# Layer 0 of a two-block transformer kernel: the v blocks first, q and k by pairs of heads, the attention steps woven between their half blocks, and the head's first weights in column parts

## What is computed

```
cond = silu(c)                                    # c: (1, 1024)
mod = cond @ ada_w[0] + ada_b[0]                  # ada_w[0]: (1024, 6144)
sh1, sc1, g1, sh2, sc2, g2 = split(mod, 6)
h = rms_norm(x, norm1_g[0]) * (1 + sc1) + sh1
q, k, v = split(h @ diff_w_in, 3)                 # diff_w_in: (1024, 3072); 8 heads
s = q_m . k_m / 8   for the two maps m of a head  # 64 features each; ALiBi, chunk-causal mask
a = softmax(s_0) - lam * softmax(s_1)             # lam from four vectors of 64
o = rms_norm(a @ v, subln_g) * 0.2
x = x + g1 * (o @ diff_w_out)
h = rms_norm(x, norm2_g[0]) * (1 + sc2) + sh2
x = x + g2 * moe(h)                               # 32 experts, top 2, 6 MB of weights each
```

## Time and profile before

| what | value |
|---|---|
| median of 3 runs | 1855.09 us (1849.57 to 1863.38) |
| profiled execution | 1853.06 us |
| its span, first to last instruction | 1851.3 us |
| mean granted TensorE clock | 0.971 of full speed |
| busy PE / DVE / ACT / POOL | 91% / 26% / 24% / 9% of the span |
| DMA, whole span | 585 MB, mean 316 GB/s |

### The profile page before, as it was taken

One profiled execution on the slowest core, in us unless ns is written; L12 is line 12 of the kernel. 1 busy time (PEld: TensorE's weight loads), 2 busy tenths in 40 slices (PEclk: granted clock), 3 DMA queues, 4 the chain that ended last, 5 costly groups with the idle time before them and its releaser, 6 DMA issues.

```text
span 1851.3 us, 18408 instructions
## 1 busy us (share of the span) xinstructions
PE 1687.5 (91%) x7485; PEld 858.7 (46%) x7485; DVE 489.6 (26%) x931; ACT 444.1 (24%) x939; POOL 158.1 (9%) x235
## 2 busy tenths in 40 slices
PE   5997999889888878989999999999998899989988
PEld 2843543333333334835464444444443356565564
DVE  1357220000000103244241002221120123553362
ACT  2015221111111102015231112334331034343351
POOL 2012010000000010113000010000000000100000
PEclk9998999999989999999989999999998999999999
DMA  9999779999999999987369989999999962413310
GB/s 348 360 350 401 277 278 419 421 421 420 421 421 419 420 413 397 338 349 239 109 259 389 369 298 404 393 414 420 420 420 409 377 230 100 148 53 117 137 46 24
DMA packets 119488, 585.12 MB, mean 316 GB/s; under 512 B 11744, under 2 KB 16680, under 8 KB 94720
## 3 DMA queue, kind: packets, MB, share of 16 engines
q1 hardware_dynamic: 97776, 489.59, 66.0%
q0 software_dynamic: 21504, 88.72, 13.1%
q10 hardware_dynamic: 112, 5.51, 0.8%
HBM read 578.87 MB, written 21.32 MB: 324 GB/s over the span
## 4 chain that ended last, share of the span: by engine, by line
PE 58%; DMA 29%; DVE 6%; ACT 3%; issue 3%; SPq 1%; ACTq 0%; DVEq 0%
PE psum L2179 55%; DMA ring<-in_expert_w_up 20%; DMA work<-in_ada_w 4%; DMA ring<-in_diff_w_in 2%; DVE work L1859 1%; PE psum L697 1%; DMA ring<-in_expert_w_gate 1%; DMA work<-in_ctx 1%; DMA work<-in_w_mod 1%; DVE small L1055 1%; PE psum L2418 1%; PE psum L1196 1%; DMA ring<-in_w_out 0%; DVE work L2147 0%; DVE work L2074 0%
## 5 line engine op out<-in xcount | busy, mean ns | idle before, releaser
L2179 PE MATMUL psum<-ring,work 128*64 128x512 f32 (+5 forms) x4272 | 1092.6, 574 | 69.6 <-DMA ring<-in_expert_w_up 56.3
L2179 PEld LDWEIGHTS psum<-ring,work 128*64 128x64 f32 (+2 forms) x4272 | 422.7, 152 | 666.1 <-issue 638.0
L2179 PE MATMUL psum<-work 128*128 128x192 f32 (+9 forms) x1048 | 220.4, 375 | 8.5 <-DVE work L2007 3.0
L2179 PEld LDWEIGHTS psum<-work 128*128 128x128 f32 (+3 forms) x1048 | 146.5, 191 | 108.0 <-issue 86.9
L2074 DVE TENSOR_TENSOR work<-work,psum 128x256 f32<-128x256 f32 x64 | 26.9, 421 | 593.2 <-ACT work L1779 593.2
L1779 ACT ACTIVATE work<-psum 128x256 f32<-128x256 f32 x64 | 24.5, 383 | 607.4 <-PE psum L2179 607.4
L2179 PE MATMUL psum<-work,ring 128*128 128x256 f32 x704 | 156.1, 381 | 3.5 <-DMA ring<-in_diff_w_in 2.0
L2179 PEld LDWEIGHTS psum<-work,ring 128*128 128x128 f32 x704 | 132.0, 190 | 27.8 <-issue 7.0
L1646 ACT ACTIVATE work<-psum 128x256 f32<-128x256 f32 (+5 forms) x184 | 79.7, 443 | 225.0 <-PE psum L2418 76.0
L1545 POOL DMA_INDIRECT expert_rows<-work,targets x56 | 55.1, 984 | 807.1 <-DVE work L2100 807.1
L2100 DVE TENSOR_TENSOR work<-psum,rows 128x512 f32<-128x512 f32 x64 | 44.3, 692 | 255.8 <-PE psum L2179 255.7
(11 more groups left out here) (293 smaller groups left out, 956.3 us busy)
## 6 DMA issues: line engine op xcount, KB each, us to landing
ring<-in_expert_w_gate SPq DMA_DIRECT2D x60, 2048.0 KB, 16.5
ring<-in_expert_w_up SPq DMA_DIRECT2D x60, 2048.0 KB, 17.2
ring<-in_expert_w_down SPq DMA_DIRECT2D x57, 2048.0 KB, 13.5
work<-in_ada_w POOLq DMA_DIRECT2D x40, 1024.0 KB, 8.0
ring<-in_w_in SPq DMA_DIRECT2D x12, 2048.0 KB, 8.8
work<-in_w_mod POOLq DMA_DIRECT2D x16, 1024.0 KB, 7.9
ring<-in_diff_w_in SPq DMA_DIRECT2D x6, 2048.0 KB, 38.2
ring<-in_sb_w_in SPq DMA_DIRECT2D x6, 2048.0 KB, 22.8
```

The source lines that it names most:

```text
L2179: return T.matmul(out_, lhsT, rhs, start=start, stop=stop, skip_group_check=True)
```

## The change

Four parts, all in layer 0 (the rest of the diff renumbers counts that other lines wait for).

1. *Head in column parts.* The `first_in` columns are loaded in two halves a=0,1 (each with 512 columns of shift and 512 of scale), in pairs of row groups: 16 loads of 0.5 MB. `x` comes ahead of them. Between the halves come the first four row groups of the first two v blocks (two loads of 1 MB, `w_first`). Gain and shift of features 0 to 511 are ready before those of 512 to 1023, so the v blocks begin on half of `hT` (`head`, `first_product`, `v_part`). POOL issues its first ada loads when all head parts have landed, and loads the lambda vectors later.
2. *Order of the blocks.* v0 v1 q0 k0 q1 k1 (`SLICES`). Item 8 (q1) and those behind it wait for `ada_used` of 6, which had no such gate.
3. *Weaving.* After v, q pair 0 and k pair 0, rounds k = 0 to 11 of the attention each begin with a half block (16 trace matmuls of 256 columns) of the coming q or k pair. The scores of these rounds use one pair of banks instead of two, so the scores of round k wait for `a_max` of round k-1; the lags are 2 and 3 instead of 3 and 4. Group 2's running sum is put into DVE's attention rounds (`SUM_AT`), and item 7's product into round 0.
4. *Ada items.* Items 16 to 19 lie in rounds 13, 15, 17 and 19, items 20 and 21 behind the last round, items 22 to 27 in the projection (two behind each of its first three blocks), 28 to 31 as before.

The core of the diff:

```diff
+    FIRST_TURN = (4, 5, 6, 4)
+    SLICES = (4, 5, 0, 2, 1, 3)
+    V_BLOCKS = (0, 2, 1, 3)
+    WOVEN = 12
+    def diff_bank(u):
+        return 2 * (u % 2) if u >= WOVEN else 0
@@ SP
+            if l == 0 and n == 4:
+                sp.wait_ge(sem("ada_used"), 6)
-        for t in range(KT):
-            sp.dma_start(first_in(t), first[:, t, :]).then_inc(sem(f"first_in{t}"), 16)
-            if t == 2:
-                sp.dma_start(cst[:], a["consts"]).then_inc(sem("consts"), 16)
-                sp.dma_start(x[:], a["x"][0].rearrange("(t p) d -> p t d", p=P)).then_inc(sem("x_in"), 16)
+        sp.dma_start(x[:], a["x"][0].rearrange("(t p) d -> p t d", p=P)).then_inc(sem("x_in"), 16)
+        for a_ in range(2):
+            for q in range(4):
+                for t in range(2):
+                    sp.dma_start(first_in(a_, q)[:, t * 1024:(t + 1) * 1024].rearrange("p (s n) -> p s n", s=2),
+                                 first[:, 2 * q + t, :, a_, :]).then_inc(sem(f"first_in{4 * a_ + q}"), 16)
+                if a_ == 0 and q == 1:
+                    sp.dma_start(cst[:], a["consts"]).then_inc(sem("consts"), 16)
+            if a_ == 0:
+                for n in range(2):
+                    w = a["diff_w_in"][0][:, SLICES[n] * 512:(SLICES[n] + 1) * 512].rearrange("(t p) n -> p t n", t=KT)
+                    sp.dma_start(wslot(L_BASE[0] + n, KT, 512)[:, 0:4, :], w[:, 0:4, :]).then_inc(sem("w_first"), 16)
@@ POOL
+        pool.wait_ge(sem("first_in7"), 32)
+        for i in range(3):
+            ada_load(i)
+        pool.wait_ge(sem("first_mm"), 2)
@@ DVE
+                SUM_AT = (1, 2, 4, 5, 7, 8, 10, 11)
...
                 for k in range(16 + 2):
-                    if k == 11:
-                        ada_take(3)
+                    if 1 <= k <= WOVEN:
+                        diff_combine(k - 1)
                     if k < 16:
                         diff_scores(k)
-                    if k >= 2:
+                    if k >= WOVEN + 2:
                         diff_combine(k - 2)
+                    if k == 1:
+                        ada_take(1)
+                    if k in SUM_AT:
+                        ada_sum(2, [SUM_AT.index(k)])
+                    if k == WOVEN:
+                        ada_take(2)
@@ PE
+        def woven_half(p, c):
+            j = (p - 4) // 2
+            n = L_BASE[0] + 2 + p % 2 + 2 * (j // 2)
+            if c == 0:
+                loaded(pe, n)
+                pe.wait_ge(sem("qkv"), (2, 4)[p % 2] if p < 6 else p - 1)
+            w = wslot(n, KT, 512)
+            col = j % 2 * 256 + c * P
+            for t in range(KT):
+                ins = mm(bank[2 + p % 2][:, c * S:(c + 1) * S], w[:, t, col:col + P], hT[:, t, :], t == 0, t == KT - 1)
...
+        def head():
+            pe.wait_ge(sem("cond"), 1)
+            pe.wait_ge(sem("line_zero"), 1)
+            first_product(0, range(0, 4))
+            pe.wait_ge(sem("consts"), 16)
+            pe.wait_ge(sem("h_done"), TT)
+            first_turn(range(0, 6))
+            first_product(0, range(4, 6))
+            keep_warm(0, 2)
+            first_product(0, range(6, KT))
+            first_cols(0)
+            keep_warm(0, 5)
+            for i, b in enumerate(V_BLOCKS):
+                if i == 0:
+                    pe.wait_ge(sem("w_first"), 32)
+                v_part(b, range(0, 4))
+                if i == 0:
+                    first_turn(range(6, KT))
+                elif i == 1:
+                    first_product(1, range(0, KT))
+                elif i == 2:
+                    first_cols(1)
+            for i, b in enumerate(V_BLOCKS):
+                if i % 2 == 0:
+                    loaded(pe, L_BASE[0] + b % 2)
+                ins = v_part(b, range(4, KT))
...
-        DIFF_ITEMS = share_out(16, [0, 0] + 8 * [1] + [0, 0] + 4 * [1, 0])
+        DIFF_ITEMS = [[KT - 1] if k == 0 else [2 * KT - 1] if k == WOVEN else [(k + 19) // 2] if k in (13, 15, 17, 19) else []
+                      for k in range(16 + 4)]
+        PROJ_ITEMS = [[22, 23], [24, 25], [26, 27], []]
         def diff_attention():
-            pe.wait_ge(sem("qkv"), 12)
             for k in range(16 + 4):
+                if k < WOVEN:
+                    woven_half(6 + k // 2, k % 2)
                 if k < 16:
                     hd, qt = k // 2, k % 2
                     nk = S if qt else P
-                    if k >= 2:
-                        pe.wait_ge(sem("a_max"), k - 1)
+                    pe.wait_ge(sem("qkv"), 6 + 2 * (k // 4))
+                    if k:
+                        pe.wait_ge(sem("a_max"), k if k <= WOVEN else k - 1)
```

More of the change, by code:

```diff
@@ L1487, in ada_load @@
             if i >= 3:
-                pool.wait_ge(sem("ada_used"), i - 1 if group_of(i - 3) in SUMMED and (i - 3) % KT < KT - 1 else i - 2)
+                before = group_of(i - 3)
+                if before in SUMMED and (i - 3) % KT == KT - 2:
+                    pool.wait_ge(sem("ada_sum"), SUMMED.index(before) + 1)
+                else:
+                    pool.wait_ge(sem("ada_used"), i - 1 if before in SUMMED and (i - 3) % KT < KT - 2 else i - 2)
             for k, n, which, c in runs(g):
@@ L1795, in _ @@
             take_hT(2 * l)
-            take_qkv(l)
+            if l:
+                take_qkv(l)
             if l == 0:
                 act.preload_act_table_set("natural_log_exp_and_others")
+                for p in range(6):
+                    take_woven(p)
                 act.wait_ge(sem("lam_dot"), 1)
@@ L1849, in gain_cols, with ada_sum @@
             link(V.scalar_tensor_tensor(gain, gain, 1.0, g_, ALU.add, ALU.mult))
-        def ada_sum(g):
-            for t in range(KT):
+        def ada_sum(g, ts=range(KT)):
+            for t in ts:
                 i = KT * (g - 1) + t
@@ new lines, in first_turn, with first_cols @@
+        def first_turn(ts):
+            for t in ts:
+                for tile in range(TT):
+                    ins = T.transpose(bank[FIRST_TURN[t // 2]][:, (t % 2 * TT + tile) * P:(t % 2 * TT + tile + 1) * P],
+                                      h[:, tile, t * P:(t + 1) * P], ident)
+                if t % 2:
+                    ins.then_inc(sem("hT_mm"), 1)
+        def first_cols(a_):
+            pe.wait_ge(sem("first_line"), 2 * a_ + 1)
+            for i in range(2):
+                ins = T.transpose(bank[(3, 5)[a_]][:, i * P:(i + 1) * P], line[:, a_ * S + i * P:a_ * S + (i + 1) * P], ident)
+            ins.then_inc(sem("first_mm"), 1)
@@ new lines, in head @@
+        def head():
[24 more added lines that the diff above has]
+                ins = v_part(b, range(4, KT))
+                if i % 2:
+                    taken(ins, L_BASE[0] + b % 2)
+                else:
+                    ins.then_inc(sem("qkv_mm"), 1)
+            for p in (4, 5):
+                for c in range(2):
+                    woven_half(p, c)
```

209 lines of the change are left out of this document (129 added, 80 removed).

## The result

The changed kernel takes 1859.88 us (median of 20 runs, 1854.77 to 1865.58), the kernel before 1854.53 us beside it (20 runs, 1849.57 to 1863.38). The ratio is 1.003, with a 95% interval of 1.0019 to 1.0041: 5 us slower, where 6.5 us of gain were forecast. The profiled execution took 1858.52 us against 1853.06, its span 1856.7 us, at the same mean clock of 0.971.

The account below looks back on a forecast made before the run. PE bounds up to about 300 us, then DMA waits for expert weights until layer 0 ends near 727 us. PE's path allows 6 us, the bytes 15; 1853.06 - 6.5 = 1846.5 us, range 1835 to 1857.

Parts of the forecast that it names:

- Head: Start of layer 0: v blocks begin at 28 us instead of 39.85; half-megabyte parts cost nothing, bounds 0 and +2 us.
- the forecast's 75: End of PE's v, first q and k products and transposes: 75 us, where the same products ended at 82 before.
- waits about a microsecond for the last part: PE's only wait counted before 75 us: about a microsecond for the last part of the head's second half.
- Round 0: First attention round: PE waits 3.5 us for item 7's sum, until 82 us; bounds no wait or 7 us.
- Woven rounds: Attention rounds 1 to 11: 4.9 us each, 54 us in all, ending at 137 us; bounds 4.7 and 5.9 a round.
- Rival (2): DVE bounds the woven rounds, 1 us a round, 11 us in all: total 1851 us; chance 0.2 shared with another rival.
- Rounds 12 to 19: Last attention rounds: round 13 begins at 141 us, projection at 164.5 us, 20.5 us earlier; bounds 161 and 175.
- Projection: Projection to transposes: 37.2 us of work plus 8 us of late ada loads; transposes at 210 us, 6 us ahead.
- rival (3): Projection's ada loads all take 28.2 us: +10 us, 1863 us; gain turns to loss over 17 us each; chance 0.1.
- Router and first gathers: Between transposes and first expert: 27 us as before, first expert at 237 instead of 243.1 us.
- The bytes: DMA up to the experts: 58 MB by 174 us, 98 MB by 275 us instead of 290, allowing 15 us.
- The smaller decides: Of the bytes' 15 us and PE's path's 6 us, the smaller sets the gain, taken as 6.5 us.

Follow-up runs that it names:

- the router edit: Changed kernel with layer 0's four router loads issued behind ada load 10 instead of 4: 1853.85 us, ratio 1.0016 to the kernel before.
- gate 16: Changed kernel with the gate of the expert stream at `ada_used` 16 instead of 24: 1868.21 us, ratio 1.007 to the kernel before.

## Why the prediction was wrong

*Head.* v was to begin at 28 us and began at 25.95. The lambda loads are gone from the start: DMA moves 402 GB/s from 10 to 15 us, where the kernel before had 229. The half-megabyte parts were priced at nothing, with bounds of 0 and 2 us. The window of this stretch gives 391 GB/s:

```profile
5.00:40.00 35.00, 24.25 (x179) 11.56 (x180) 3.17 (x9) 5.99 (x11) 1.65 (x3) 1.00 1.05 391
```

From 15 to 35 us alone it is 387 GB/s, in packets of 2.0 KB in the mean, where the kernel before had 416 from its 1 MB loads. That is 7%, about 1.5 us on 8.4 MB: inside the bounds, though not nothing. The Trainium skill's 1 MiB advice (DMA: Bandwidth & Descriptors, section Bandwidth), by which the prediction estimated a loss of at least 4 us, is not borne out here, where 16 such loads were queued together. Its figures are for loads that GpSimd issues, and these were issued by SyncE. The pair's block of q ended at 67.80 us; with 7.1 us for that of k that would be 74.9 us, the forecast's 75.

*k0's weights.* This step failed first. "waits about a microsecond for the last part" was all that the prediction had for waits in the head, and nothing for k0: its 2 MB, asked for at 34.5 us, landed at 77.2. What was missing was the neighbourhood. POOL's lambda and router loads, moved by the change to 52 to 59 us, fell on SP's loads of q and k, beside two ada loads (51.94 and 55.19 us). The windows of this stretch:

```profile
60.00:65.00 5.00, 4.70 (x21) 3.88 (x21) 2.19 (x1) 0.60 (x1) 0.54 (x1) 1.00 0.92 217
65.00:70.00 5.00, 2.81 (x13) 2.12 (x12) 1.43 (x1) 0.60 (x1) 0.00 (x0) 1.00 1.13 272
70.00:75.00 5.00, 0.00 (x0) 0.00 (x0) 0.92 (x1) 0.00 (x0) 0.53 (x1) 0.64 0.78 280
75.00:80.00 5.00, 2.77 (x7) 2.24 (x8) 3.92 (x2) 0.00 (x0) 0.53 (x1) 0.50 0.42 136
```

DMA is busy (0.92, 1.13) but moves only 217 and 272 GB/s, against 365 in the mean of the same 80 us before. The same ten microseconds with the router edit, and then with the lambda loads taken away too:

```profile
60.00:65.00 5.00, 4.70 (x22) 3.95 (x22) 2.07 (x1) 0.60 (x1) 0.54 (x1) 1.00 0.81 229
65.00:70.00 5.00, 2.71 (x13) 2.05 (x11) 1.36 (x1) 0.60 (x1) 0.00 (x0) 1.00 0.94 381
```

```profile
60.00:65.00 5.00, 4.85 (x12) 2.14 (x12) 0.42 (x1) 1.19 (x2) 0.53 (x1) 1.00 1.04 409
65.00:70.00 5.00, 4.70 (x17) 2.71 (x16) 3.75 (x2) 0.60 (x1) 0.53 (x1) 1.00 0.94 343
```

So the slow stretch from 65 to 70 us belongs to the router loads (272 GB/s become 381) and the one from 60 to 65 us to the lambda loads (229 become 409, in a kernel that is 5 us later here). The diff was read for order, and the moved small loads were seen ("37 us if the small lambda loads, now later, had taken room"), but only their absence from the head was counted, not their cost at the new place. PE stood idle from 67.8 to 77.2 us, and the granted clock fell from 1.00 to 0.64 and 0.50; the first matmuls behind the wait ran at the lower level.

*Round 0.* Forecast to end its wait for item 7 at 82 us; the sum ended at 89.0 us, and the product stands at 90.39. PE, late through k0, came only when the sum was there. But the small loads had delayed this chain as well: with the router loads away the sum ended at 84.7 us. Round 1 began at 91.36 us, 8.4 us later than the 83 us taken, and beyond the bounds of that step.

*Woven rounds.* 4.9 us each with bounds of 4.7 and 5.9; they took 51.5 us for eleven, 4.7 us each. DVE fitted, and one pair of banks cost nothing. Rival (2) is refuted for this kernel.

*Rounds 12 to 19.* From the end of the woven rounds to the projection 27.5 us were forecast, 28.4 us measured. So the projection's start, 171.3 instead of 164.5 us, is the late round 0 (+8.4), less the faster rounds (-2.5), plus 0.9.

*Projection.* This is the second step that failed, and the larger. "With 11 to 13.4 us a load" gave waits of 2, 5 and 1 us. The landing times of the eight w_mod loads, as in the earlier trace rows, and then of the one issued at 188.8 us:

```profile
DMA to landing us min/median/max: 7.1/15.8/25.4
...
DMA to landing us min/median/max: 25.4/25.4/25.4
```

The loads of items 25 to 27 took 18.9 to 25.4 us. That there would be waits here was foreseen, their size wasn't: 10.4 us for item 25, 3.5 for item 27 and none for item 30, 13.9 us instead of 2, 5 and 1. For item 25 alone that is five times the forecast. The cost of the lower clock behind the waits was missing altogether: from the projection's start to the transposes 55.7 us passed, which is 37.2 us of work as forecast, 13.9 us of waits and 4.6 us more, of which the matmul rows behind the waits show 4.4 as longer than at full clock (the granted clock was 0.82 and 0.87). The mechanism is that of rival (3), whose turning point was put at "over 17 us each"; the loads that counted were above it. It had a chance of 0.1 because 28.2 us was one load of eight in the earlier trace rows. But six of eight now had company, which the prediction itself said. The median of a quiet stage was used for loads moved into a crowded one.

*Router and first gathers.* 27 us forecast, 27.1 us measured.

*The bytes.* 58 MB by the opening of the gate at 174 us were forecast; the windows give 56 MB there, and the gate opened at 180.49 us. The idle time from 200 us on was found, and used (share 0.96 instead of 0.55). But DMA moved less elsewhere: 2.6 MB up to 80 us, 0.7 up to 115, 3.8 up to 175 (share 0.88), 1.6 up to 200 and 3.5 from 250 to 290 us (0.69), against 7.8 MB more between 200 and 250 us. From 80 to 175 us items 10 and 11 and the experts are held back by gates on ada items, which now come later (items 10 and 11 went out at 127.4 us); from 250 us on slots come free at PE's pace. So by 290 us 4.3 MB less than before had been moved, not more. This step failed as well: it promised 15 us and cost 10.2 by the rate of the experts' regime. "The smaller decides" took the two paths as independent, and the table above shows that they aren't. The sum also took 6.5 us where its own PE path gave 6.1, which changes nothing.

*The wait in `ada_load`.* It wasn't in the prediction at all: the part of the diff beyond the four listed changes was taken for renumbering, and the text on the change says so, wrongly. It is worth 7.8 us in the changed kernel (from the start of layer 1 to the long part of its projection 160.0 us, 167.8 with the old wait there). Without it the error would have been about 20 us. So the forecast came as near as it did by luck: its error in layer 0 was 17 us.

The sum: the first expert 17.1 us later than the forecast 237 (6.8 before the projection, 10.3 in it), at layer 1's start 17.4 us, less 6.9 us in layer 1, plus 1.4 us behind it: 12 us between 1846.5 and 1858.5.

## What to carry to other kernels

Before work is moved into another stage, price its loads by the rows that lie in company there, not by the median of all, and follow every small load that changes its place to whatever big transfer it will meet. Where DMA is nearly always busy, a faster order of engine work can turn into waits. Look first for a load held back by a semaphore that it doesn't need: one such line was worth 8 us here, and the reordering none. Compare the bytes moved up to a common point before the engines' own starts. A line of a diff that looks like bookkeeping but changes what a load waits for belongs in the sum.

## What was unexpected of the hardware

A high DMA share doesn't mean that much is moved: from 60 to 70 us the share was 0.92 and 1.13 at only 217 and 272 GB/s. Moving the four router loads (162 KB together) away from there brought a 2 MB load on another queue forward by 4.3 us (9.42 to 5.09 us of wait, of which some 2 us vary). The five lambda loads (under 130 KB) delayed the head by 5.3 us when they were issued at its start. What it is in them that costs, small rows, their number or their queue, was not tried.

A 1 MB load of w_mod took 5.1 us at the least (gate 16) and up to 25.4 us in the changed kernel, beside four 2 MB loads and a copy of 5.4 MB. With the copy moved in the old order, the longest fell from 28.2 to 14.7 us. And PE's waits of over 9 us were paid for twice: around the 9.42 us of idling the granted clock read 0.64 and 0.50, and behind the 10.40 us a block of 7.13 us took 9.04.
